# First slab with its low-input pass last, the first sum of squares in four large operations, and own PSUM banks for the second slab pair of a hybrid decoder layer

## The reference, cut to what matters here

```python
def rmsnorm(x, g):
    xf = x.astype(F32)
    y = xf * lax.rsqrt(jnp.mean(xf * xf, axis=-1, keepdims=True) + EPS)
    return (y * g.astype(F32)).astype(x.dtype)

def half_ffn(h, g, w_in, w_out):     # D_MODEL = 2048, D_FF = 5632
    u = rmsnorm(h, g) @ w_in
    a, b = jnp.split(u, 2, axis=-1)
    return h + 0.5 * ((jax.nn.silu(a) * b) @ w_out)
```

## Time and profile before

| | |
|---|---|
| time, median of 3 runs | 2543.26 us (2542.37, 2543.26, 2546.80) |
| span of the profiled execution | 2545.1 us (its own time outside the trace is not listed apart) |
| TensorE matmul busy | 2457.1 us, 97% |
| TensorE weight loads busy | 2387.9 us, 94% |
| VectorE busy | 1370.0 us, 54% |
| ScalarE busy | 985.8 us, 39% |
| GpSimd busy | 183.1 us, 7% |

### The profile page before, as it was taken

The page is one execution under the profiler, slowest core; times in us unless marked ns, Lnnn a source line. Parts: engine busy times, 40 slices in busy tenths (PEclk is TensorE's granted clock), DMA queues, the critical chain, the costliest instruction groups (busy, mean ns, idle before and its releaser), DMA issues.

```text
span 2545.1 us, 47205 instructions
## 1 busy us (share of the span) xinstructions
PE 2457.1 (97%) x19106; PEld 2387.9 (94%) x19106; DVE 1370.0 (54%) x1567; ACT 985.8 (39%) x1036; POOL 183.1 (7%) x198
## 2 busy tenths in 40 slices
PE   7999999999999999975999999999999999999997
PEld 6999999999999998874888898999999999999997
DVE  6554554555556545531556456565555555555554
ACT  4333333333333344441555453344333333333332
POOL 2000000000005100011000012021000000000015
PEclk9999999999999999985998899999999999999998
DMA  5445445445444443351221354555545555545444
GB/s 179 178 152 180 175 155 180 172 158 179 171 171 159 171 165 116 118 131 58 68 81 66 133 207 154 179 179 176 176 168 191 180 168 195 181 162 197 177 169 138
DMA packets 70901, 401.78 MB, mean 158 GB/s; under 512 B 12498, under 2 KB 15218, under 8 KB 35488
## 3 DMA queue, kind: packets, MB, share of 16 engines
q1 hardware_dynamic: 62960, 386.86, 43.9%
q0 software_dynamic: 7872, 13.94, 2.0%
HBM read 391.43 MB, written 9.27 MB: 157 GB/s over the span
## 4 chain that ended last, share of the span: by engine, by line
PE 89%; issue 5%; DVE 3%; POOL 1%; ACT 1%; DMA 0%; DVEq 0%; SPq 0%; POOLq 0%; ACTq 0%
PE bank L1343 28%; PE bank L1349 28%; PE bank L1344 27%; PE bank L386 1%; PE bank L407 1%; PE bank L425 1%; DVE w_lo L948 1%; ACT w_hi L625 1%; DVE x_lo L953 0%; PE bank L1457 0%; PE bank L423 0%; PE bank L370 0%; PE bank L1515 0%; POOL scratch L603 0%; PE bank L1564 0%
## 5 line engine op out<-in xcount | busy, mean ns | idle before, releaser
L625 ACT ACTIVATE w_hi<-raw 128x2048 fp32r<-128x2048 f32 (+1 forms) x404 | 705.4, 1746 | 1248.7 <-PE bank L1349 1210.7
L948 DVE TENSOR_TENSOR w_lo<-raw,w_hi 128x2048 fp32r<-128x2048 f32 (+1 forms) x404 | 844.7, 2091 | 464.3 <-ACT w_hi L625 464.3
L1343 PE MATMUL bank<-x_hi,w_hi 128*128 128x264 f32 (+1 forms) x3456 | 908.1, 296 | 16.7 <-DVE x_lo L953 11.7
L1344 PE MATMUL bank<-x_lo,w_hi 128*128 128x264 f32 (+1 forms) x3456 | 889.6, 290 | 0.0
L1343 PEld LDWEIGHTS bank<-x_hi,w_hi 128*128 128x128 f32 x3456 | 659.2, 191 | 40.8 <-issue 19.6
L1344 PEld LDWEIGHTS bank<-x_lo,w_hi 128*128 128x128 f32 x3456 | 659.5, 191 | 0.0
L1343 PE MATMUL bank<-y_hi,w_hi 128*128 128x264 f32 (+1 forms) x2368 | 598.2, 288 | 6.1 <-DVE y_lo L1246 5.6
L1344 PE MATMUL bank<-y_lo,w_hi 128*128 128x264 f32 (+1 forms) x2368 | 596.7, 287 | 0.0
L1349 PE MATMUL bank<-x_hi,w_lo 128*128 128x264 f32 (+1 forms) x3456 | 493.0, 292 | 0.0
L1349 PEld LDWEIGHTS bank<-x_hi,w_lo 128*128 128x128 f32 x3456 | 457.2, 191 | 3.9 <-issue 2.3
L1343 PEld LDWEIGHTS bank<-y_hi,w_hi 128*128 128x128 f32 x2368 | 447.2, 189 | 7.5 <-DVE y_lo L1246 6.9
(11 more groups left out here) (247 smaller groups left out, 1255.8 us busy)
## 6 DMA issues: line engine op xcount, KB each, us to landing
raw<-in_w_in SPq DMA_DIRECT2D x176, 1024.0 KB, 4.8
raw<-in_w_out SPq DMA_DIRECT2D x128, 704.0 KB, 4.0
raw<-in_w_proj SPq DMA_DIRECT2D x52, 1024.0 KB, 4.8
raw<-in_w_merge SPq DMA_DIRECT2D x32, 1024.0 KB, 4.8
raw<-in_w_o SPq DMA_DIRECT2D x16, 1024.0 KB, 4.8
scratch<-in_state_in POOLq DMA_DIRECT2D x8, 512.0 KB, 5.4
out_state_s<-scratch POOLq DMA_DIRECT2D x8, 512.0 KB, 5.4
hT<-in_xT SPq DMA_DIRECT2D x4, 560.0 KB, 7.4
```

Of the source, the lines that this page charges most:

```text
L625: act.activation(w_hi[:, b, 0:kt * P], raw[:, b, 0:kt * P], ACT.Copy).then_inc(hi_split, 1)
L948: dve.tensor_tensor(w_lo[:, b, 0:kt * P], raw[:, b, 0:kt * P], w_hi[:, b, 0:kt * P].bitcast(F32), ALU.subtract).then_inc(lo_split, 1)
L1343: pe.matmul(out, w, x[0][:, k, 0:T], start=(k == ks[0]), stop=False)
L1344: pe.matmul(out, w, x[1][:, k, 0:T], start=False, stop=False)
```

## The change

Five edits, all around the first two pairs.

1. `first_slab` replaces `product` for slab (0,0): all 16 `w_hi` by `x_hi` matmuls, each waiting only for its high tile, then the 16 with `w_lo`, then the 16 with `x_lo`, each waiting for its low tile.
2. The first sum of squares leaves GpSimd. ScalarE squares the whole of `hT` in one operation of 128 x 4480 into `x_sq`, and VectorE folds it by three additions (2240, 1120, 560 columns). TensorE adds the last two tiles by its two `ones` matmuls.
3. Pair 1 is written out, and its products go to banks 2 and 3, without a wait for `bank_free`. The loop starts at pair 2.
4. In pair 0 ScalarE and VectorE make both weight parts of pair 1 ahead of the square root and the reciprocal.
5. `x_sq` lies over `ga_raw`, so the transfer of `ga_raw` moves from the start to the end of the first FFN, beside those of `dist0` and `dist1`, and ScalarE's wait there is for all three.

```diff
--- before.py
+++ after.py
@@ -126,7 +126,7 @@
         acc, sq, std = (at(TA * i, TA) for i in range(5, 8))
-        acc2, sq2 = act_a, b_n
+        x_sq = at(TA * 8, KD * TA)
         ga_raw = at(3060, GA_COLS)
@@ -468,6 +467,8 @@
                     load_pairs(w_out[c], h + FC, KD // 2, FC)
             ffn(t["w1_in"], t["w1_out"], 0, first=True)
+            sp.wait_ge(sumsq_done, 1)
+            sp.dma_start(ga_raw, t["w_ga"]).then_inc(tables_loaded, 16)
             sp.dma_start(dist0, t["c_dist0"]).then_inc(tables_loaded, 16)
@@ -496,23 +497,14 @@
...
-                pool.tensor_tensor(acc[:, 0:T], acc[:, 0:T], sq[:, 0:T], ALU.add).then_inc(acc_done, tiles)
-
-
-            zero_acc(0)
-            for m in range(0, KD, 2):
-                pool.wait_ge(x_loaded[m // 4], 16)
-                if m:
-                    pool.wait_ge(acc_done, m)
-                add_square(hT[:, m, :], m // 2 + 1, TA, tiles=2)
+                pool.tensor_tensor(acc[:, 0:T], acc[:, 0:T], sq[:, 0:T], ALU.add).then_inc(acc_done, 1)
@@ -643,10 +635,12 @@
                         half, f = h0 + i, f0 + c * FC + i
                         split_hi(half + 1, 0, kt_next)
                         if first:
+                            if r == 0:
+                                split_hi(half + 1, 1, kt_next)
                             root(r, T)
                         act.wait_ge(bank_free, 2 * half + 1)
                         act.activation(sig[:, 0:T], a_n[:, 0:T], ACT.Sigmoid).then_inc(sig_done, 1)
-                        if not last_inner:
+                        if not last_inner and not (first and r == 0):
                             split_hi(half + 1, 1, kt_next)
                         act.wait_ge(s_done, f + 1)
@@ -655,7 +649,9 @@
                     if c == 0:
                         inner(0, KD, first=True)
-                    with act.Fori(1 if c == 0 else 0, FC - 1) as i:
+                    if c == 0 and r == 0:
+                        inner(1, KD)
+                    with act.Fori((2 if r == 0 else 1) if c == 0 else 0, FC - 1) as i:
                         inner(i, KD)
                     inner(FC - 1, FC, last_inner=True)
                     h1 = h0 + FC
@@ -683,9 +679,10 @@
             split_hi(0, 1, KD, first=True)
+            act.activation(x_sq, hT[:].rearrange("p a b -> p (a b)"), ACT.Square).then_inc(xsq_done, 1)
             act.wait_ge(eps_set, 1)
             ffn(0, 0, s1_hi, TA, 0, 1, x_hi)
-            act.wait_ge(tables_loaded, 16)
+            act.wait_ge(tables_loaded, 16 * 3)
             act.activation(ga_hi, ga_raw, ACT.Copy).then_inc(gahi_done, 1)
@@ -964,21 +961,24 @@
                     def inner(i, kt_next, last_inner=False, first=False):
                         half, f = h0 + i, f0 + c * FC + i
+                        own = 2 if r == 0 and c == 0 and isinstance(i, int) and i == 1 else 0
                         if first:
                             split_lo(half + 1, 0, kt_next)
+                            if r == 0:
+                                split_lo(half + 1, 1, kt_next)
                             inverse(r, T)
                         dve.wait_ge(slab_done, 2 * half + 1)
-                        dve.tensor_tensor(a_n[:, 0:T], bank[0][:, 0:T], rstd[:, 0:T], ALU.mult).then_inc(bank_free, 1)
+                        dve.tensor_tensor(a_n[:, 0:T], bank[own][:, 0:T], rstd[:, 0:T], ALU.mult).then_inc(bank_free, 1)
                         if not first:
                             split_lo(half + 1, 0, kt_next)
                         dve.wait_ge(sig_done, f + 1)
                         dve.tensor_tensor(act_a[:, 0:T], a_n[:, 0:T], sig[:, 0:T], ALU.mult).then_inc(acta_done, 1)
                         dve.wait_ge(slab_done, 2 * half + 2)
-                        dve.tensor_tensor(b_n[:, 0:T], bank[1][:, 0:T], rstd[:, 0:T], ALU.mult).then_inc(bank_free, 1)
+                        dve.tensor_tensor(b_n[:, 0:T], bank[own + 1][:, 0:T], rstd[:, 0:T], ALU.mult).then_inc(bank_free, 1)
                         dve.wait_ge(bank_free, 2 * half + 2)
                         dve.wait_ge(acta_done, f + 1)
                         dve.tensor_tensor(s32[:, 0:T], act_a[:, 0:T], b_n[:, 0:T], ALU.mult).then_inc(s_done, 1)
-                        if not last_inner:
+                        if not last_inner and not (first and r == 0):
                             split_lo(half + 1, 1, kt_next)
                         dve.wait_ge(shi_done, f + 1)
                         dve.tensor_tensor(s_lo[:, bass.ds(i, 1), 0:T], s32[:, 0:T],
@@ -1020,13 +1022,12 @@
             split_lo(0, 1, KD)
-            dve.tensor_tensor(acc2, hT[:, 1], hT[:, 1], ALU.mult).then_inc(acc2_done, 1)
-            for n in range(1, KD // 2):
-                dve.tensor_tensor(sq2, hT[:, 2 * n + 1], hT[:, 2 * n + 1], ALU.mult).then_inc(sq2_done, 1)
-                dve.wait_ge(sq2_done, n)
-                dve.wait_ge(acc2_done, n)
-                dve.tensor_tensor(acc2, acc2, sq2, ALU.add).then_inc(acc2_done, 1)
-                dve.wait_ge(acc2_done, n + 1)
+            dve.wait_ge(xsq_done, 1)
+            for n, half_of in enumerate((8, 4, 2)):
+                if n:
+                    dve.wait_ge(xsum_done, n)
+                dve.tensor_tensor(x_sq[:, 0:half_of * TA], x_sq[:, 0:half_of * TA], x_sq[:, half_of * TA:2 * half_of * TA],
+                                  ALU.add).then_inc(xsum_done, 1)
             ffn(0, 0, s1_hi, s1_lo, TA, 0, 1, (x_hi, x_lo))
             dve.wait_ge(gahi_done, 1)
             dve.tensor_tensor(ga_lo, ga_raw, ga_hi.bitcast(F32), ALU.subtract).then_inc(galo_done, 1)
@@ -1357,12 +1358,28 @@
                 product(bank[b][:, 0:T], b, range(kt), x, T, 2 * half + b, ready, beside).then_inc(slab_done, 1)
             def sum_squares(r, T):
-                pe.wait_ge(acc_done, KD * (r + 1))
                 if r == 0:
                     pe.wait_ge(consts_loaded, 16 * N_CONST)
-                    pe.wait_ge(acc2_done, KD // 2)
-                    pe.matmul(bank[7][:, 0:T], ones[:], acc2[:, 0:T], start=True, stop=False)
-                pe.matmul(bank[7][:, 0:T], ones[:], acc[:, 0:T], start=(r > 0), stop=True).then_inc(sumsq_done, 1)
+                    pe.wait_ge(xsum_done, 3)
+                    pe.matmul(bank[7][:, 0:T], ones[:], x_sq[:, 0:T], start=True, stop=False)
+                    pe.matmul(bank[7][:, 0:T], ones[:], x_sq[:, T:2 * T], start=False, stop=True).then_inc(sumsq_done, 1)
+                else:
+                    pe.wait_ge(acc_done, KD * r)
+                    pe.matmul(bank[7][:, 0:T], ones[:], acc[:, 0:T], start=True, stop=True).then_inc(sumsq_done, 1)
+
+            def first_slab(x, T):
+                out = bank[0][:, 0:T]
+                pe.wait_ge(hi_split, 1)
+                for k in range(KD):
+                    pe.wait_ge(xhi_done, k + 1)
+                    pe.matmul(out, w_hi[:, 0, k * P:(k + 1) * P], x[0][:, k, 0:T], start=(k == 0), stop=False)
+                pe.wait_ge(lo_split, 1)
+                for k in range(KD):
+                    pe.matmul(out, w_lo[:, 0, k * P:(k + 1) * P], x[0][:, k, 0:T], start=False, stop=False)
+                for k in range(KD):
+                    pe.wait_ge(xlo_done, k + 1)
+                    last = pe.matmul(out, w_hi[:, 0, k * P:(k + 1) * P], x[1][:, k, 0:T], start=False, stop=(k == KD - 1))
+                last.then_inc(slab_done, 1)
             def tiles_of_norm(r):
                 def ready(k):
@@ -1373,13 +1390,17 @@
                 for c in range(CH):
                     h0 = half0 + c * (FC + KD // 2)
                     i0 = 0
-                    if c == 0:
-                        slab(h0, 0, KD, x, T, ready=tiles_of_norm(r), first=half0 == 0)
-                        if r:
-                            sum_squares(r, T)
-                        slab(h0, 1, KD, x, T, first=half0 == 0)
-                        if not r:
-                            sum_squares(r, T)
+                    if c == 0 and r == 0:
+                        first_slab(x, T)
+                        slab(h0, 1, KD, x, T, first=True)
+                        sum_squares(0, T)
+                        for b in range(2):
+                            product(bank[2 + b][:, 0:T], b, range(KD), x, T, 2 * (h0 + 1) + b).then_inc(slab_done, 1)
+                        i0 = 2
+                    elif c == 0:
+                        slab(h0, 0, KD, x, T, ready=tiles_of_norm(r))
+                        sum_squares(r, T)
+                        slab(h0, 1, KD, x, T)
                         i0 = 1
                     with pe.Fori(i0, FC) as i:
                         for b in range(2):
```

More of the change, by code:

```diff
@@ L498, in zero_acc, with add_square @@
             def zero_acc(r):
-                if r:
-                    pool.wait_ge(sumsq_done, r)
+                pool.wait_ge(sumsq_done, r)
                 pool.memset(acc, 0.0).then_inc(acc_zero, 1)
-                pool.wait_ge(acc_zero, r + 1)
```

(15 more changed lines are left out.)

7 lines of the change are left out of this document (3 added, 4 removed).

## The result

Measured in one comparison of ten runs each, the changed kernel took 2532.81 us in the median (2522.95 to 2534.18), the kernel before 2542.90 (2536.69 to 2551.79). The ratio is 0.9946, with an interval of 0.9933 to 0.9959: 10 us by the medians (their ratio is 0.9960), 13.7 by the ratio times 2542.9. The two differ because the runs are uneven: three of the changed kernel's lie at 2522.95 to 2525.39 and three of the kernel before's at 2550.80 to 2551.79, which moves the means (2530.35 and 2544.60, ratio 0.9944) and not the medians.

What follows compares the result with a forecast made beforehand. At the start, VectorE's chain (low tiles, weight splits, squares and sums) was taken to hold TensorE up. 4.6 us on slab (0,0) plus 5.0 up to (1,0)'s end make 9.6, giving 2533.6 us, range 2530 to 2537.5.

Steps and rivals of the forecast that it cites:

- Low tiles: VectorE's low input tiles at the start: with GpSimd quiet, 0.44 to 0.46 us apart instead of 0.81.
- Rival A: Start: low tiles stay slow at 0.81 us, gain only 5.9 to 7.7 us, time about 2536.5; 8%.
- Slab (0,0): TensorE's first slab: ends at 21.4 instead of 26.0, a gain of 4.6 us (4.0 to 5.1).
- Slab (0,1), the sums, pair 1: After the first slab: no waits, square 3.9 us, additions 4.6, `ones` matmuls 1.1; (1,0) ends at 34.9 instead of 44.51.
- The 3.4 and the 1.6: Before and in (1,0): TensorE's 3.4 us pause and the 1.6 us clock drop go, together 5.0 us.
- The stall's next place: Slab (2,0): the now later norm chain ends at 37.5, before TensorE needs it at 41.1; 3.6 us to spare.
- The loop's start: TensorE's first loop, entered at 41.1 without a pause: entering costs nothing.
- the moved transfer: Table load moved to the first FFN's end: lands at 832.7, used at 844.91, 12 us to spare, costs nothing.
- rival B: A wait no longer covered, code fetch at the loop's start or late sums: gain 6.2 to 9 us, about 2536; 7%.
- D: Slower: grown TensorE code makes the two FFNs' loops pause each turn; about 2555 us at 0.15 a turn; 3%.
- rival C: Behind the start: the gain doesn't arrive, since a transfer that comes no earlier is waited for; time 2543; 4%.
- later stages hang on TensorE's position alone: Everything after the start: the 9.6 us gained there is carried unchanged to the kernel's end.

Runs made afterwards that it cites:

- busy_gpsimd: Changed kernel with GpSimd's 16 squares and sums put back, on tiles that nothing reads; 2534.27 us, ratio 0.9961 to the kernel before.
- again: The changed kernel, unaltered, run once more in alternation with the kernel before; 2532.68 us, ratio 0.9963.
- filled_after: Changed kernel with 330 extra matmuls in TensorE's mixer pause ahead of the scan; 2534.36 us, ratio 0.9963 to the kernel before.
- banks_only: Kernel before with only own banks for pair 1 and both its weight splits ahead of the root; 2537.97 us, ratio 0.9976.
- filled_before: Kernel before with 330 extra matmuls in TensorE's mixer pause ahead of the scan; 2543.13 us, ratio 0.9997.
- squares_only: Kernel before with only the square moved to ScalarE, additions to VectorE, and x_sq in ga_raw's place; 2536.05 us, ratio 0.9970.
- old_order: Changed kernel with the first slab's passes interleaved again, waiting for the low tiles; 2530.49 us, ratio 0.9950 to the kernel before.

## Why the prediction was right or wrong, point by point

The mechanism was right in every part. Two things of the sum failed: the size of one term, slab (0,0), and what was put at nothing, the clock later in the kernel.

**Low tiles.** Right: 0.42 to 0.43 apart, forecast 0.44 to 0.46. GpSimd as the cause is shown by busy_gpsimd. The trace agrees with the rule of the Trainium skill, page "SBUF — State Buffer", section "Who interferes with whom": two SBUF inputs on VectorE beside reads by GpSimd. Rival A's time for the (1,0) end, 36.8 to 38.6, was met by that kernel just under its lower end: 34.58 + 2.06 = 36.6.

**Slab (0,0)**, "Gain on this slab 26.0 - 21.4 = 4.6 us (4.0 to 5.1)". This is the term that was mis-sized. Its last pass began at 18.61 and 16 x 0.129 later it was over, at 20.7: 5.3 gained, 6.6 in the profile of "again" (17.29 + 2.06 = 19.35), 4.8 in filled_after (19.20 + 2.06 = 21.26). I took the delay of the clock's rise as 3.4, between two rows, 1.8 and 4.8 after the last wait, and counted it from 15.75. Measured, the clock rose at 17.7: about 9.3 of the second pass's 16 matmuls 0.233 apart and the rest 0.129 make the 3.03 us from 15.58 to 18.61. That is a delay of 2.0. My lower bound was also added up wrong: a delay of 1.8 gives an end of 20.7, not the 20.9 that stands there, so the gain's upper bound was 5.3 by my own terms. In "again" the whole second pass ran at full clock:

```profile
15.23 2.23 PE L1378 MATMUL bank<-x_hi,w_lo 128*128 128x280 f32 x16
17.29 2.23 PE L1381 MATMUL bank<-x_lo,w_hi 128*128 128x280 f32 x16
```

So the clock can rise before the last wait ends, which my way of counting ruled out, and the bound of 5.1 was too low by 1.5. The end of slab (0,0) before wanders too: it is 26.00, 26.49 and 26.8 in the profiles of before, banks_only and filled_before, which have the same code there.

**Slab (0,1), the sums, pair 1.** Right, but for a small step, once the shift of 0.7 is taken off: 6.18 for (0,1), the square 3.93 (forecast 3.9) with no table load, the additions 4.62 (4.6) and over at 25.4 (25.5), TensorE's first sum at 26.84 without a wait, the loads and the splits in time. The two `ones` matmuls take 0.74 from the first one's start to (1,0)'s, not 1.1, and (1,0) is over at 33.96, not 34.9. "The 3.4 and the 1.6" are 5.0; from the end of slab (0,0) to the mark it is 5.2, here as in banks_only. So the gain at the mark is 5.3 + 5.2 where the sum had 4.6 + 5.0.

**The stall's next place.** Right: the root at 30.44, `a_n` of pair 1 at 36.31 + 0.44 = 36.75, where (2,0) begins at 38.08 + 2.06 = 40.1. Of the 3.6 forecast 3.4 are left. The table loads are 1.28 here as before; the 2.66 of the Trainium skill's page "ScalarE: Activation LUTs", section "What ACT_TABLE_LOAD costs", is not to be seen between L617's end and the root, which are 29.02 and 30.44.

**The loop's start, the moved transfer.** Right: (2,0)'s third pass begins 6.18 behind (1,1)'s (44.26 and 38.08), so rival B falls, and D with it: the last 983 us, which hold the second FFN, are equal to 0.02, and the first FFN's lose nothing, as the next row shows. The tables' first use, 844.91 before, is now:

```profile
834.37 0.49 ACT L686 ACTIVATE small_r<-scratch 128x368 fp32r<-128x368 f32 x1
```

10.54 earlier, exactly the mark's gain, so the 800 us between lose nothing, against rival C.

**Edit 1.** I booked all of slab (0,0)'s gain without saying which edit earns it. The runs say edit 2 does (squares_only, 5.2 on that slab): with the low tiles 0.42 apart the interleaved order keeps up with them.

**The time.** Forecast 2533.6, measured medians 2532.81 and 2532.68. That they are so near is in part luck: the start gave 10.5 to 11.9 instead of 9.6, and the changed kernel's mean is 2530.35. By the first comparison's ratio the time is 0.9946 x 2543.26 = 2529.5 (2526.2 to 2532.8), half a microsecond below my range. The step that failed beside slab (0,0) is that the sum stops at the start ("later stages hang on TensorE's position alone") and allows only "3 us for the runs' spread". Three runs of before, 2542.4 to 2546.8, had told too little: in 51 later runs before spreads over 2536.96 to 2552.26, and the changed kernel's ten over 11 us. Of the 13.5 between the first two profiles the start gave 10.5 and the scan's clock 2.9. Most of the spread lies in the scan. Over the fourteen profiles the stretch of the scan takes 376.0 to 385.1 us, the mixer ahead of it (from the row above at 834.37 to the scan) 328.9 to 332.3, and what follows the scan 982.7 to 983.0. In old_order's profile, at 2526.27 us, the scan reads:

```profile
1165.46:1541.48 376.02, 369.15 (x2744) 329.60 (x2743) 214.75 (x297) 186.66 (x256) 37.08 (x49) 0.91 0.31 110
```

9 us less than before at a clock of 0.91 instead of 0.88. What decides in an execution how long the clock stays low there is open: it changes between executions of one kernel, and the filling did not steady it. Such swings are large enough for the 3 us by which the first comparison's ratio exceeds the start's gain. That they are its cause is shown for the profiled runs, and for the others only by their mean clock.
